# First loads and set-up of three attention programs: keys ahead of the bias, first queries from ScalarE's queue, second slot set up in the loop

## The chip, the core and the metric

The kernel runs on one core of a Trainium2 chip. The metric is the device time of one execution in microseconds (us); before the change it is 4377.17 us, the median of 3 runs from 4371.15 to 4381.04.

## What is computed

One step of a two-layer streaming encoder: 2048 frames of a new stream and 64 frames of a continued one. The first layer has 8 heads of group A (each chunk of 64 frames reads itself and eight chunks back, with a relative bias) and 8 heads of B (a frame reads all frames up to itself, with a forgetting term in the logits). The second has 8 heads of C (window of two chunks back, two key groups, a sink in the softmax) and 8 heads of D (one shared key and value, 256 selected keys for each frame).

```python
def attend(q, k, v, bias, mask, sink=None):
    s = jnp.einsum('bqhgd,bkhd->bhgqk', qg, k).astype(F32) * (d ** -0.5)
    s = s.reshape(b, hq, tq, -1) + bias
    s = jnp.where(mask, s, NEG_INF)
    ...
    o = jnp.einsum('bhgqk,bkhd->bqhgd', p, v)
...
    oa = chunk_band_prompt(qa, ka, va, A_BACK_CHUNKS, bias_a)
    ob = forget_prompt(qb, kb, vb, logf)
    mix = jnp.concatenate([oa * jax.nn.silu(ga), ob * jax.nn.silu(gb)], axis=-1)
    return x + mix @ w_out, new
```

## The kernel before

The kernel is a sequence of programs, with a barrier of all engines between two of them: projections, the attention of A and B (`attention_by_keys`), the output of the first layer, projections and selection of the second, the attention of C, then of D (`attention_by_blocks`, called once for each), and the output of the second layer. Each program writes what every engine does in its own order; engines wait for each other by counting semaphores. An engine runs its instructions in that order, so whatever stands behind a wait waits too. SP, ScalarE and GpSimd also issue DMAs, each on a queue of its own.

**A and B.** Sixteen heads run one after the other, each in one of two slots (`k_a`, `k_b`, `c_a`, `c_b`, `q_a`, `q_b`, `v`, `v_c`, with index head mod 2). A matrix of keys or queries is loaded as float32 into one of two `raw` buffers (`item_loads`: item 0 the keys, 1 the queries, 2 the cached keys, each in two halves of 64 partitions), rounded on ScalarE into the `_a` tile (`round_item`), and what rounding left is kept: for keys on GpSimd (`split_keys`, L859), for queries on VectorE (`split_queries`, a product into `q_b`, L848, and the remainder into `q_a`, L851). A score is then two matmuls. The rows 64 to 67 of the `_b` tiles hold ones that carry the softmax shift and the forgetting term. VectorE sets them up before the first head (L1166 to L1184): memsets of both slots, then, when the identity has come, `shown` and a product of each key tile with it (L1181), and a rounded identity (`ident_r`). Then it keeps the turned bias (`keep_bias`), and splits the first queries. TensorE turns the bias of a head against the identity (`turn_bias`), forms the maxima's scores (`maximum`, L951 and L952) into two banks, which VectorE reduces (`reduce`, L1112), and later the transposed scores (`scores`), which VectorE biases (`add_bias`), ScalarE exponentiates (`exponent`) and TensorE multiplies with the values (`values`). `KeyPlan` cuts this into chunks: the loop over `c` does scores two chunks ahead and maxima five.

**C and D.** Blocks of 128 queries, all heads of a block together. `key_loads` fills a `raw` buffer with the keys of one group (item 0), the cached keys (item 1), and for C the second group (2 and 3); items 2 and 3 wait until items 0 and 1 are split. `query_loads` loads one block of queries in four DMAs of 128 KB. VectorE waits for all three constants (identity, bias, and sinks in C or a bfloat16 identity in D: `consts` up to `N_CONST` = 48), keeps the turned bias (`keep_bias`), splits the first keys (`split_keys`, L1752) and then the queries. GpSimd issues the loads of the values once the tiles are set up (`fixed`), prepares a block (`prepare`, and for D `add_near`); in D it waits for the kept bias first.

## Time and profile before

| | before |
|---|---|
| median of 3 runs | 4377.17 us |
| lowest and highest | 4371.15 and 4381.04 us |
| the profiled execution, its own time | 4374.29 us |
| its span, first to last instruction | 4372.5 us |
| TensorE matmuls, busy | 3836.7 us, 88% of the span |
| VectorE, ScalarE, GpSimd, busy | 2250.8, 1593.5 and 682.4 us (51%, 36%, 16%) |
| granted TensorE clock, mean | 0.945 |

The profile is one execution. A busy share is an average over the whole span; the programs differ, so the heads of the programs are read from their own stretch. In the table by stretch the five busy times are those of TensorE's matmuls, its weight loads, VectorE, ScalarE and GpSimd, each with its instructions. An idle time stands in square brackets in a timeline row, with what ended it behind the arrow. The attention of A and B starts at 943.5 us of the span, that of C at 3164.5 and that of D at 3369.7.

### The profile page before, as it was taken

What the parts mean: (1) busy time and instruction counts of PE and PEld (TensorE: products, weight loads), DVE (VectorE), ACT (ScalarE), POOL (GpSimd) and SP (SyncE); (2) the same over time, 40 slices, a digit from 0 to 9 for tenths busy, and PEclk for the clock granted to TensorE, in tenths of its full rate; (3) what the DMA queues carried; (4) which work ended last, traced back from release to release, by engine and by line L of the source; (5) the groups of instructions that cost most, each with busy time, mean ns of one, the idle gap of its engine ahead of it and who ended that gap; (6) DMA issues with size and microseconds to landing.
All of it is one profiled execution on the core that took longest, in us unless ns stands there. A gap on an engine that the chain in (4) does not pass through costs nothing. (4 is left out here: it accounts for less than half of the span.)

```text
span 4372.5 us, 51419 instructions
## 1 busy us (share of the span) xinstructions
PE 3836.7 (88%) x18129; PEld 2643.7 (60%) x18129; DVE 2250.8 (51%) x4858; ACT 1593.5 (36%) x2424; POOL 682.4 (16%) x408
## 2 busy tenths in 40 slices
PE   5999999968888999996998779889877699999698
PEld 3789988966666566564874544443344455555376
DVE  7211111137776444443230199999678876666332
ACT  3100001104444334333320189995345333333333
POOL 3100000011212111111430000000032632211133
PEclk8999999989999999998999899999979799999899
DMA  5221122133334223212431211111243210100243
GB/s 184 69 73 67 63 73 81 65 84 82 92 91 99 63 60 74 64 36 91 160 126 63 63 38 57 56 58 48 80 104 94 61 39 23 25 21 3 97 154 125
DMA packets 222512, 328.51 MB, mean 75 GB/s; under 512 B 22224, under 2 KB 129032, under 8 KB 220896
## 3 DMA queue, kind: packets, MB, share of 16 engines
q1 hardware_dynamic: 173280, 236.21, 18.9%
q10 hardware_dynamic: 43776, 72.50, 4.5%
q0 software_dynamic: 5216, 16.70, 1.8%
q8 instruction: 138, 2.26, 0.2%
q14 instruction: 102, 0.84, 0.1%
HBM read 214.35 MB, written 110.99 MB: 74 GB/s over the span
## 5 line engine op out<-in xcount | busy, mean ns | idle before, releaser
L1017 PE MATMUL attAB_p_o<-attAB_pt,attAB_v 128*65 128x512 f32 (+3 forms) x1120 | 441.3, 492 | 3.0 <-ACT attAB_pt L1064 3.0
L1104 DVE TENSOR_REDUCE attAB_mx<-attAB_p_s 128x1 f32<-128x512 f32 (+2 forms) x360 | 210.7, 608 | 313.1 <-PE attAB_p_s L952 200.6
L497 DVE COPY ab_stage<-ab_pA 128x256 f32<-128x256 f32 (+1 forms) x108 | 56.5, 523 | 603.5 <-PE ab_pA L466 579.4
L2360 DVE TENSOR_SCALAR_CACHE_REDUCE cd_junk<-score,cd_thr 128x512 bf16<-128x512 f32 (+8 forms) x288 | 350.3, 1274 | 1.4 <-DVE cd_thr L2377 0.3
L2398 ACT ACTIVATE cd_gate<-score,cd_thr 128x384 bf16<-128x384 f32 (+2 forms) x192 | 322.3, 1679 | 23.3 <-DVE cd_thr L2377 16.1
L994 PE MATMUL attAB_p_t<-attAB_q_a,attAB_k_a 128*128 128x512 f32 (+3 forms) x560 | 314.0, 564 | 0.0
L464 PE MATMUL ab_pA<-ab_W_hi,h_hi 128*128 128x256 f32 x1088 | 309.0, 284 | 3.3 <-PE ab_pA L466 3.2
L465 PE MATMUL ab_pA<-ab_W_lo,h_hi 128*128 128x256 f32 x1088 | 307.9, 283 | 0.0
L466 PE MATMUL ab_pA<-ab_W_hi,h_lo 128*128 128x256 f32 x1088 | 307.8, 283 | 0.0
L495 ACT ACTIVATE ab_stage<-ab_pA 128x256 f32<-128x256 f32 (+1 forms) x108 | 50.1, 464 | 700.3 <-PE ab_pA L466 669.5
L1625 PE MATMUL attD_p_o<-attD_pt,attD_v 128*65 128x512 f32 x548 | 287.6, 606 | 0.0
L369 PE MATMUL cd_pA<-hT_cd,cd_W 128*128 128x512 f32 (+1 forms) x640 | 245.5, 544 | 39.0 <-ACT cd_stage L2561 26.7
L464 PE MATMUL ab_pA<-h_hi,ab_W_hi 128*128 128x512 f32 (+1 forms) x640 | 238.4, 373 | 14.1 <-ACTq L482 5.0
L372 PE MATMUL cd_pA<-cd_W,hT_cd 128*128 128x512 f32 x544 | 237.9, 599 | 13.7 <-ACT cd_stage L2561 13.3
L951 PE MATMUL attAB_p_s<-attAB_k_a,attAB_q_a 128*128 128x384 f32 (+3 forms) x560 | 209.1, 375 | 41.3 <-DVE attAB_mx L1112 22.1
L465 PE MATMUL ab_pA<-h_lo,ab_W_hi 128*128 128x512 f32 (+1 forms) x640 | 237.4, 371 | 0.0
L466 PE MATMUL ab_pA<-h_hi,ab_W_lo 128*128 128x512 f32 (+1 forms) x640 | 237.3, 371 | 0.0
L1603 PE MATMUL attD_p_t<-attD_q_a,attD_k_a 128*128 128x512 f32 x274 | 203.5, 743 | 26.1 <-DVE attD_s_t L1824 26.0
L1064 ACT ACTIVATE attAB_pt<-attAB_p_t 128x512 f32<-128x512 f32 (+2 forms) x328 | 175.9, 566 | 138.4 <-PE attAB_p_t L995 134.7
L2076 PE MATMUL mix_pY<-mix_W_hi,mix_m_hi 128*128 128x512 f32 x544 | 218.4, 402 | 0.0
L369 PEld LDWEIGHTS cd_pA<-hT_cd,cd_W 128*128 128x128 f32 x640 | 114.8, 197 | 169.7 <-issue 123.7
L2077 PE MATMUL mix_pY<-mix_W_lo,mix_m_hi 128*128 128x512 f32 x544 | 215.4, 396 | 0.0
(343 smaller groups left out, 8809.4 us busy)
## 6 DMA issues: line engine op xcount, KB each, us to landing
attAB_raw<-t_k SPq DMA_DIRECT2D x32, 640.0 KB, 7.3
attAB_raw<-t_q SPq DMA_DIRECT2D x32, 640.0 KB, 9.7
t_qg<-cd_stage SPq DMA_DIRECT2D x74, 256.0 KB, 2.0
ab_W_raw<-in_w_ab SPq DMA_DIRECT2D x17, 1024.0 KB, 5.8
mix_o<-t_o SPq DMA_DIRECT2D x34, 512.0 KB, 4.3
t_q<-ab_stage ACTq DMA_DIRECT2D x40, 256.0 KB, 2.0
t_k<-ab_stage ACTq DMA_DIRECT2D x40, 256.0 KB, 2.0
norm_x<-in_x ACTq DMA_DIRECT2D x17, 512.0 KB, 3.6
```

Of the source, the lines that this page charges most:

```text
L369: last = nc.tensor.matmul(pA[s][:, 0:w], W[j % 2][:, k, c * P:(c + 1) * P], hT[:, k, r * BANK:r * BANK + w], start=(k == 0), stop=(k == KT ...
L372: last = nc.tensor.matmul(pA[s][:, 0:w], hT[:, k, r * P:(r + 1) * P], W[j % 2][:, k, 0:w], start=(k == 0), stop=(k == KT - 1))
L464: nc.tensor.matmul(out, lh, rh, start=(k == 0), stop=False)
L465: nc.tensor.matmul(out, lh, rl, start=False, stop=False)
L466: last = nc.tensor.matmul(out, ll, rh, start=False, stop=(k == KT - 1))
L994: nc.tensor.matmul(out, hi[:, ks], q_a[j][:, cols], start=(x == 0), stop=False)
L1017: done = nc.tensor.matmul(p_o[u % 2][0:VW, i0 * P:(i0 + n) * P], left, pt[c % NPT][:, at * P:(at + n) * P], start=(c == plan.chunks_of[u][ ...
L1625: nc.tensor.matmul(p_o[u % 2][0:VW, :], left, pt[c % NPT][:], start=(c == first), stop=(c == last)).then_inc(valued, 1)
L2076: nc.tensor.matmul(out, m_hi[s][:, k, :], W_hi[:, k, cols], start=(k == 0), stop=False)
L2077: nc.tensor.matmul(out, m_hi[s][:, k, :], W_lo[:, k, cols], start=False, stop=False)
L2360: nc.vector.tensor_scalar(junk[nth % 2][:, 0:widths[n]], sc[n][:], T[:, n:n + 1], None, ALU.is_ge, ALU.add, accum_out=cnt[s % 2][:, n:n + ...
L2398: nc.scalar.activation(gate[:, 0:widths[n]], sc[n][:], ACT.Sign, bias=T[:, n:n + 1], accum_out=cnt[s % 2][:, n:n + 1]).then_inc(signed, 1)
```

## The change

In A and B, SP issues the identity and then the first keys, ahead of the first bias; the first queries are issued by ScalarE. VectorE sets up the first slot before the loop, with the rounded identity ahead of the key tiles' rest; the seven instructions for the second slot go into steps 0 to 5 of the loop (`fix_second`), and what reads the second slot waits for a new semaphore. TensorE turns the first bias before it waits for the set-up. In C and D, SP issues the first keys behind the identity and ahead of the bias and the third constant; the first two blocks of queries are issued by ScalarE, before its first wait.

```diff
--- before.py
+++ after.py
@@ -780,9 +780,10 @@
         row_turned, row_kept, bias_turned, bias_kept, bias_laid, t_biased = (sem(n) for n in (
             "row_turned", "row_kept", "bias_turned", "bias_kept", "bias_laid", "t_biased"))
         bias_in = [sem(f"bias_in{k}") for k in pair]
-        ident_in = sem("ident_in")
+        ident_in, second_fixed = sem("ident_in"), sem("second_fixed")
         ITEMS = 3
-        FIXED = 2 * 5 + 2 + 2 + 4
+        FIXED = 5 + 2 + 2 + 2
+        SECOND = 5 + 2
         span = lambda h: plan.last_of_head[h] + 1 - plan.first_of_head[h]
 
         places = {plan.first_of_head[h] + span(h) * (1 + 2 * n) // 9: (h + 1, n) for h in range(NH - 1) for n in range(ITEMS)}
@@ -844,6 +845,10 @@
         def split_queries(dve, h):
 
             j, m = h % 2, ITEMS * h + 1
+            if h == 0:
+                dve.wait_ge(fixed, FIXED)
+            if h == 1:
+                dve.wait_ge(second_fixed, SECOND)
             dve.wait_ge(rounded, m + 1)
             nc.vector.tensor_scalar(q_b[j][0:FORGET, :], q_a[j][0:FORGET, :].bitcast(F32), only_q[0:FORGET, 0:1], None,
                                     ALU.mult).then_inc(copied, 1)
@@ -877,11 +882,13 @@
             @block.sync
             def _(sp):
                 sp.dma_start(ident[:], d.ident).then_inc(ident_in, 16)
+                item_loads(sp, 0, 0)
                 for h in range(NH):
                     if kinds[h] == "A":
                         bias_loads(sp, h)
                     for n in range(ITEMS):
-                        item_loads(sp, h, n)
+                        if h or n == 2:
+                            item_loads(sp, h, n)
                         if h == 0 and n == 1:
                             for dst, src in ((identb, d.identb), (tri, d.tri), (tri_t, d.tri_t)):
                                 sp.dma_start(dst[:], src).then_inc(consts, 16)
@@ -929,6 +936,8 @@
                     if m == 0 or plan.units[plan.maxima[m - 1][0]][0] != h:
                         pe.wait_ge(k_split, 2 * h + 1)
                         pe.wait_ge(q_split, h + 1)
+                        if h == 1:
+                            pe.wait_ge(second_fixed, SECOND)
                         if h == HEADS:
                             pe.wait_ge(consts, 48)
                         if kinds[h] == "B":
@@ -1027,9 +1036,9 @@
                     done.then_inc(turned, 1)
 
                 pe.wait_ge(ident_in, 16)
+                turn_bias(0)
                 pe.wait_ge(fixed, FIXED)
                 pe.wait_ge(ident_kept, 2)
-                turn_bias(0)
                 for n, u in enumerate(plan.early):
                     for m in plan.max_of[u]:
                         maximum(m)
@@ -1078,6 +1087,7 @@
                         act.wait_ge(turned, u - 1)
                     nc.scalar.activation(o_t[u % 2][:, 0:w], p_o[u % 2][0:VW, 0:w], ACT.Copy).then_inc(o_kept, 1)
 
+                item_loads(act, 0, 1)
                 for n in range(ITEMS):
                     round_item(act, 0, n)
                 for u in plan.early:
@@ -1128,6 +1138,19 @@
                     dve.wait_ge(negated, 2 * u + 2)
                     nc.vector.tensor_tensor(lo, nm[u % 2][:, 0:n, :], hi.bitcast(F32), ALU.subtract).then_inc(shifted, 1)
 
+                def fix_second(x):
+
+                    if x < 3:
+                        nc.vector.memset((k_b, c_b, q_b)[x][1][HD:AUX, :].bitcast(F32), 1.0).then_inc(second_fixed, 1)
+                    elif x == 3:
+                        nc.vector.memset(v[1][:, :, HD:VW], 1.0).then_inc(second_fixed, 1)
+                        nc.vector.memset(v_c[1][:, :, HD:VW], 1.0).then_inc(second_fixed, 1)
+                    else:
+                        tile = (k_b, c_b)[x - 4]
+                        dve.wait_ge(second_fixed, x - 3)
+                        nc.vector.tensor_scalar(tile[1][HD:AUX, :], tile[1][HD:AUX, :].bitcast(F32), shown[HD:AUX, 0:1], None,
+                                                ALU.mult).then_inc(second_fixed, 1)
+
                 def keep_bias(h):
                     j = h % 2
                     for x, w in enumerate((BANK, P)):
@@ -1162,26 +1185,23 @@
                                             view[:, 0:n, 0:HD], rs[u % 2][:, 0:n, :].broadcast_to([P, n, HD]), ALU.mult
                                             ).then_inc(o_out, 1)
 
-                for j in pair:
-                    nc.vector.memset(k_b[j][HD:AUX, :].bitcast(F32), 1.0).then_inc(fixed, 1)
-                    nc.vector.memset(c_b[j][HD:AUX, :].bitcast(F32), 1.0).then_inc(fixed, 1)
-                    nc.vector.memset(q_b[j][HD:AUX, :].bitcast(F32), 1.0).then_inc(fixed, 1)
-                    nc.vector.memset(v[j][:, :, HD:VW], 1.0).then_inc(fixed, 1)
-                    nc.vector.memset(v_c[j][:, :, HD:VW], 1.0).then_inc(fixed, 1)
+                nc.vector.memset(k_b[0][HD:AUX, :].bitcast(F32), 1.0).then_inc(fixed, 1)
+                nc.vector.memset(q_b[0][HD:AUX, :].bitcast(F32), 1.0).then_inc(fixed, 1)
                 for k in pair:
                     nc.vector.memset(shift[k][:].bitcast(F32), 0.0).then_inc(fixed, 1)
                 nc.vector.memset(only_q[0:HD, :], 1.0).then_inc(fixed, 1)
                 nc.vector.memset(only_q[HD:AUX, :], 0.0).then_inc(fixed, 1)
                 dve.wait_ge(ident_in, 16)
+                nc.vector.tensor_copy(ident_r[:], ident[:]).then_inc(ident_kept, 1)
                 nc.vector.tensor_reduce(shown[HD:AUX, :], ident[HD:AUX, HD:FORGET], AX.X, ALU.max).then_inc(ident_kept, 1)
-                dve.wait_ge(ident_kept, 1)
-                dve.wait_ge(fixed, FIXED - 4)
-                for tile, w in ((k_b, ROWS), (c_b, WIDEST * P)):
-                    for j in pair:
-                        nc.vector.tensor_scalar(tile[j][HD:AUX, :], tile[j][HD:AUX, :].bitcast(F32), shown[HD:AUX, 0:1], None,
-                                                ALU.mult).then_inc(fixed, 1)
-                dve.wait_ge(fixed, FIXED)
-                nc.vector.tensor_copy(ident_r[:], ident[:]).then_inc(ident_kept, 1)
+                nc.vector.memset(c_b[0][HD:AUX, :].bitcast(F32), 1.0).then_inc(fixed, 1)
+                nc.vector.memset(v[0][:, :, HD:VW], 1.0).then_inc(fixed, 1)
+                nc.vector.memset(v_c[0][:, :, HD:VW], 1.0).then_inc(fixed, 1)
+                dve.wait_ge(ident_kept, 2)
+                dve.wait_ge(fixed, FIXED - 2)
+                for tile in (k_b, c_b):
+                    nc.vector.tensor_scalar(tile[0][HD:AUX, :], tile[0][HD:AUX, :].bitcast(F32), shown[HD:AUX, 0:1], None,
+                                            ALU.mult).then_inc(fixed, 1)
                 keep_bias(0)
                 split_queries(dve, 0)
                 for u in plan.early:
@@ -1193,6 +1213,8 @@
                 for c in range(NT):
                     if c + 2 < NT and kind_of(c + 2) == "A":
                         add_bias(c + 2)
+                    if c < 6:
+                        fix_second(c)
                     for m in plan.max_at[c]:
                         reduce(m)
                         if m == plan.max_of[plan.maxima[m][0]][-1]:
@@ -1436,17 +1458,15 @@
             @block.sync
             def _(sp):
                 sp.dma_start(ident[:], d.ident).then_inc(consts, 16)
+                key_loads(sp, 0)
                 sp.dma_start(bias[:], (d.bias_c if kind == "C" else d.bias_d).rearrange("h p n -> p h n")).then_inc(consts, 16)
                 if kind == "C":
                     sp.dma_start(sink[:], d.sinks.broadcast_to([P, HEADS])).then_inc(consts, 16)
                 else:
                     sp.dma_start(identb[:], d.identb).then_inc(consts, 16)
-                key_loads(sp, 0)
-                query_loads(sp, 0)
                 if kind == "D":
                     for b in range(NMASK):
                         mask_loads(sp, b)
-                query_loads(sp, 1)
                 for m in range(1, len(items)):
                     key_loads(sp, m)
                 for b in range(2, NRAW - 1):
@@ -1716,6 +1736,8 @@
                         act.wait_ge(turned, u - 1)
                     nc.scalar.activation(o_t[u % 2][:], p_o[u % 2][0:VW, :], ACT.Copy).then_inc(o_kept, 1)
 
+                query_loads(act, 0)
+                query_loads(act, 1)
                 act.wait_ge(fixed, FIXED)
                 round_keys(0)
                 for b in plan.early_blocks:
```

## Rows read from the trace of the kernel before

**Rows 1.** Table by stretch: window, length, five busy times, granted clock, DMA share, GB/s.
```profile
944.00:975.00 31.00, 1.30 (x5) 0.93 (x5) 27.07 (x24) 4.66 (x3) 12.66 (x7) 0.50 0.63 142
...
3164.00:3200.00 36.00, 6.99 (x31) 6.46 (x31) 16.91 (x36) 6.66 (x6) 11.48 (x9) 0.50 0.82 181
...
3369.00:3400.00 31.00, 4.82 (x22) 4.01 (x22) 16.15 (x16) 6.13 (x6) 11.95 (x7) 0.50 1.01 210
```

**Rows 2.** Timeline, head of A and B: start, duration, engine, line, out<-in, [idle before].
```profile
956.03 2.02 ACT L842 ACTIVATE attAB_k_a<-attAB_raw 128x2176 fp32r<-128x2176 f32 x1 [18.53 <-DMA attAB_raw<-t_k]
...
958.13 4.75 POOL L859 TENSOR_TENSOR attAB_k_b<-attAB_raw,attAB_k_a 64x2176 fp32r<-64x2176 f32 x1 [10.10 <-ACT attAB_k_a L842]
...
963.40 2.02 ACT L842 ACTIVATE attAB_q_a<-attAB_raw 128x2176 fp32r<-128x2176 f32 x1 [5.35 <-DMA attAB_raw<-t_q]
...
967.72 1.17 DVE L1184 CAST attAB_ident_r<-attAB_ident 128x128 fp32r<-128x128 f32 x1
...
972.48 2.61 DVE L851 SCALAR_TENSOR_TENSOR attAB_q_a<-attAB_raw,attAB_q_a 64x2176 fp32r<-64x2176 f32 x1
...
975.19 0.45 PE L951 MATMUL attAB_p_s<-attAB_k_a,attAB_q_a 128*128 128x128 f32 x1 [4.71 <-DVE attAB_q_a L851]
```

**Rows 3.** Timeline, A and B: long memsets of the set-up, idle times in the loop.
```profile
946.33 1.76 DVE L1167 MEMSET attAB_c_b<- 4x2048 f32 x1 [0.38 <-issue]
...
948.50 1.87 DVE L1168 MEMSET attAB_q_b<- 4x2176 f32 x1 [0.40 <-issue]
...
992.94 0.69 DVE L1148 TENSOR_TENSOR attAB_s_t<-attAB_p_t,attAB_bias_t 128x512 f32<-128x512 f32 x1 [2.15 <-PE attAB_p_t L995]
...
997.31 0.39 PE L951 MATMUL attAB_p_s<-attAB_k_a,attAB_q_a 128*128 128x256 f32 x1 [0.61 <-DVE attAB_mx L1112]
```

**Rows 4.** Lines L1181 and L848 by themselves: durations in ns, least/median/most, first and last start.
```profile
L1181 DVE TENSOR_SCALAR attAB_k_b<-attAB_k_b,attAB_shown x2: 1337/3474/5612, 958.4 to 964.0; 4x2176 fp32r<-4x2176 f32 x2
...
L848 DVE TENSOR_SCALAR attAB_q_b<-attAB_q_a,attAB_only_q x16: 1339/1342/1346, 971.1 to 1914.2; 66x2176 fp32r<-66x2176 f32 x16
```

**Rows 5.** DMA queues (packets, MB, share): 3155 to 3215 (GpSimd's), then 3179 to 3183.
```profile
q0 software_dynamic: 416, 1.18, 9.0%
...
q0 software_dynamic: 256, 0.79, 89.0%
q1 hardware_dynamic: 255, 0.12, 18.2%
```

**Rows 6.** Timeline, head of C, in the order of time.
```profile
3171.95 0.23 DVE L1854 CAST attC_ident_r<-attC_ident 128x128 fp32r<-128x128 f32 x1 [1.36 <-DMA attC_sink<-in_sinks]
...
3176.01 0.69 DVE L1765 COPY attC_bias_t<-attC_p_o 128x512 f32<-128x512 f32 x1 [0.16 <-PE attC_p_o L1540]
3177.91 2.02 ACT L1673 ACTIVATE attC_k_a<-attC_raw 128x2176 fp32r<-128x2176 f32 x1 [17.18 <-DMA attC_raw<-t_kq]
...
3182.40 1.28 SPq L1391 DMA_DIRECT2D attC_raw<-t_kq  x2
...
3194.02 2.02 ACT L1673 ACTIVATE attC_k_a<-attC_raw 128x2176 fp32r<-128x2176 f32 x1 [4.85 <-DMA attC_raw<-t_kq]
...
3198.63 0.45 PE L1577 MATMUL attC_p_s<-attC_k_a,attC_q_a 128*128 128x128 f32 x1 [5.69 <-DVE attC_k_b L1752]
```

**Rows 7.** Timeline, head of D, in the order of time.
```profile
3376.24 0.49 DVE L1854 CAST attD_ident_r<-attD_ident 128x128 fp32r<-128x128 f32 x1 [1.07 <-DMA attD_identb<-in_identb]
...
3384.39 2.42 DVE L1752 TENSOR_TENSOR attD_k_b<-attD_raw,attD_k_a 64x2176 fp32r<-64x2176 f32 x1 [3.13 <-ACT attD_k_a L1673]
...
3391.00 2.84 POOL L1471 TENSOR_SCALAR attD_q_b<-attD_q_a,attD_only_q 66x1024 fp32r<-66x1024 f32 x1 [12.57 <-ACT attD_q_a L1679]
...
3393.87 14.76 DVE L1758 SCALAR_TENSOR_TENSOR attD_q_a<-attD_q_raw,attD_q_a 64x1024 fp32r<-64x1024 f32 x2 [7.06 <-POOL attD_q_b L1471]
...
3403.35 7.25 POOL L1489 TENSOR_TENSOR attD_near_t<-attD_bias_t,attD_msk_t 128x1024 f32<-128x1024 f32 x3
...
3412.68 0.27 DVE L1788 CUSTOM_DVE_ANT_0 attD_junk<-attD_p_s,attD_near 128x128 bf16<-128x128 f32 x1
```

## The prediction

> **What bounds the kernel now.** By the page TensorE is busy 88% of the span, so in the long stretches the time is TensorE's, and a change at the head of a program counts by when its first matmuls of scores can run. I read the table by stretch at the three heads next [rows 1]: in the heads of A and B, of C, and of D TensorE does 1.30, 6.99 and 4.82 us of work in 31, 36 and 31 us, at a granted clock of 0.50 (the 1.2 GHz level; it had idled). VectorE is busy 27.07 of 31 us in the first, but 16.91 of 36 and 16.15 of 31 in the others, and there transfers fill the time (DMA share 0.82 and 1.01, 181 and 210 GB/s). Last, the timeline at each head.
>
> A and B [rows 2]: keys are rounded on ScalarE at 956.03, when they have landed, queries at 963.40. VectorE's set-up ends only with the cast at 967.72, so the turned bias, the split of the queries (972.48, 2.61 us) and the first matmul of scores (975.19) are late because of VectorE.
>
> C [rows 6]: the constants are there at 3171.95, the last turned bias is kept by 3176.70, and only then do the keys come (3177.91). When VectorE has split them, SP issues the keys of the second group into the freed buffer (3182.40); they are rounded at 3194.02, and TensorE goes on with the second unit at 3198.63. That load is the bound. D [rows 7]: constants at 3376.24; GpSimd starts its preparation at 3391.00 and works on to 3410.60; VectorE, held up beside it, comes to the first maximum at 3412.68.
>
> **The change part by part.** *Queries on ScalarE's queue.* They move from behind the keys to beside them. The price depends on how two queues share the DMA engines. In 4 us in which SP's and GpSimd's queues were both full, one moved 255 packets (0.12 MB), the other 256 (0.79 MB) [rows 5]: they take turns packet by packet, whatever the size. So I let ScalarE's queue add no rate and take turns with SP's, at the 210 GB/s of D's saturated head [rows 1]. By the code's access patterns the keys are 640 packets of 2 KB (1.31 MB), C's and D's two blocks of queries 2048 of 512 bytes (1.05 MB), their bias 1024 of 1 KB (1.05 MB); C's values are 416 packets, 1.18 MB [rows 5].
>
> The issues on ScalarE (two in A and B, eight in C and D, of some 0.65 us, as SP's pair of 1.28 [rows 6]) I cost at nothing: rounding waits for landed keys, and in C and D the bias comes later still. Without that cover they are 5.2 us at most. SP keeps the rest of its order; D's cached keys come one place earlier and are needed last.
>
> *Bias behind the keys, in C.* VectorE runs in order: it waits for all constants, keeps the bias, then splits the keys. Before, the bias came first and was kept 1.2 us ahead of the keys [rows 6]: free. After: the stream begins near 3166.2; the keys' 640 packets with as many of the queries are 1.64 MB, 7.8 us, so the keys land near 3174. Then 1024 packets of bias pass with 1024 of the queries and, since the values are in full turn by 3179 [rows 5], with all 416 of those: 1.05 + 0.52 + 1.18 = 2.75 MB, 13.1 us: constants near 3187. From there 4.75 us as before (3171.95 to 3176.70) and a split of 2.42 us (the same instruction in [rows 7]): buffer free at 3194.2, not 3182.4. The second group's load then finds idle engines: 1.31 MB are 6.2 us, with issue and latency some 8 us (an estimate; in the crowd of before it took 11.6), so 3202, 8 us later than 3194.02. Bounds: with the values behind the bias 1.57 MB, 7.5 us, give constants at 3181.5 and 2.7 us; with 11.6 us for the load again, 11.8 us. I take **+8**.
>
> *In D.* Keys land near 3379, but bias and identity at 3379.2 + 2.65 MB / 210 GB/s = 3392, for 3376.24. With 4.8 us as in C, GpSimd starts near 3396.8, not 3391.00, and its 19.6 us of work move by 5.8. The split of the keys (2.42 us, before in free time at 3384.39) now falls beside GpSimd, where two instructions of half that length took 14.76 us [rows 7]. Bounds: +0.6 with the values behind the bias, +8.2 with the whole split added. I take **+6**, near the shift alone, because VectorE's last pieces run after GpSimd's end either way.
>
> *A and B, head.* VectorE now sets up the first slot alone, before the loop: one of each pair of memsets and of products with the shown column goes, and the one product that ran beside GpSimd (5.61 us [rows 4]) with its hold. It is free near 956 instead of 968.9, and transfers end last: keys, queries and values are 3.29 MB, 15.7 us from 945.3, so keys and queries land together near 961 (keys 5 us later than before, queries 2.4 earlier). The bias follows 1.6 us behind and is kept by 964.7: no delay, as TensorE turns it ahead of its wait for the set-up. Keys are rounded by 963.1, queries by 965.1, and GpSimd splits the keys from 963.2 to 967.9 (its 4.75 us [rows 2]). Here VectorE's product for the queries meets GpSimd's subtraction. In all 16 heads of before it took 1.34 us; another product of its kind took 5.61 us instead of 1.34 [rows 4] when it ran beside exactly this GpSimd instruction. So I let it end at 969.2; the 2.61 us follow, and the first matmul comes at 971.9: **−3.3**. Without the hold, 969.2: −6.
>
> The Trainium skill ("SBUF — State Buffer", on the shared port pair) says that VectorE and GpSimd take that pair under an exclusive lock for a whole instruction while the other waits; by it the sum has the −3.3, by the sixteen rows the −6. The trace agrees with it in the 5.61 us.
>
> *Second slot inside the loop.* Three long memsets, two of 0.07 and two products: 1.87 + 1.76 + 1.87 + 0.14 + 2 x 1.34, with some 0.4 us of issue before each long memset [rows 3, 4], are 9.5 us. They now stand in VectorE's order between a bias addition and the maxima of steps 0 to 5. The maxima behind them free TensorE's banks, and TensorE already waits for them there (0.61 us), while VectorE has a single long idle time of 2.15 us [rows 3]. The first memset fits into that; the other 7.2 us meet two engines that wait for each other in turn. Bounds: 0, if all is taken up, and 9.5. I take **+4.5**, the middle, since neither row decides. The new waits (VectorE and TensorE for the second slot's semaphore) are over long before head 1 and cost nothing.
>
> **Sum.** −3.3 + 4.5 + 8 + 6 = +15.2 us on the profiled execution's own 4374.29 us: 4389.5, so 4389. The median shown lies 2.9 us above that execution; the range allows for it.
>
> **The rivals.** (1) *The values come behind the bias:* C +2.7, D +0.6, A and B +1.2: 4379. For it: no row fixes the values' first packet; against: 1024 packets of bias need longer than the few us of head start. (2) *The loop takes up the set-up and the hold isn't met:* A and B −6, C and D +14: 4382. For it: VectorE isn't full there; against: TensorE's waits for the maxima. (3) *Faster: ScalarE's queue brings a rate of its own.* Each queue then runs at 210 GB/s. In A and B keys land at 951.5, VectorE's set-up (956) bounds and the first matmul comes near 962, −13, of which the loop takes 4.5: −8.5. In C keys land at 3172.4 and the bias at 3177.4; the buffer is free 2 us later, but the second load meets emptier engines: 0. In D the bias lands at 3382.6 and GpSimd starts at 3387.4: −3.6. Together −12: 4362. It decides if the two hardware queues together move over 300 GB/s into the raw buffers. Against it stands the turn-taking [rows 5], though that is GpSimd's queue beside SP's, not ScalarE's.
>
> The Trainium skill ("DMA: Bandwidth & Descriptors", "Issuing engines are not separate DMA queues") says that such transfers run on the same sixteen engines and save issue time alone; by it rival (3) falls.
>
> **How the numbers follow.** Forecast 0.56, rival (1) 0.14, (2) 0.18, (3) 0.12. About 0.2% (8.8 us) is what a measurement of this kernel can tell from no change. With all terms at their upper bounds the forecast is 26 us above (4400, and 4403 with the median's 2.9); rivals (1) and (2) together are 3 us below. A little of the forecast lies within 0.2%, and so do (1) and (2): slower 0.52, same 0.36, faster 0.12. The range leaves out (3) and the far ends: 4374 to 4402.
>
> **What would show it.** Right: in C the cast of the identity some 15 us later after the program's start than now, the second keys issued near 3194 and rounded near 3202; in D GpSimd's first product 5 to 6 us later; in A and B the first matmul 3 to 4 us earlier, with memsets between the maxima and longer TensorE waits for them. Wrong: constants in C within 10 us of the keys' issue, keys that land in 6 us with queries beside them, or a loop in A and B as short as before.

## The result, and the profile after

| | before | after |
|---|---|---|
| median, us | 4377.17 | 4398.15 (4395.07 to 4411.51) |
| ratio to before | 1 | 1.0058, 95% interval 1.0043 to 1.0072 |
| profiled execution: time, span, us | 4374.29, 4372.5 | 4411.51, 4409.7 |
| first load of A and B to their last output, us | 1091.6 | 1112.8 |
| the same for C, D, us | 202.1, 737.7 | 212.4, 742.0 |

Slower, on the side I forecast, but by 21 us where the forecast (4389) lay 12 above the median. Executions of the changed kernel lie in two groups, 4395 to 4398 and 4410 to 4412, and the profiled one is of the upper; the ratio, which comes to 25 us, weighs both. In the lower group the loss is about 20 us; what lifts the other executions by some 14 us more is a question of its own, to which the experiments come back. The last three lengths are worked out from SP's first load and VectorE's last output of a program.

Head of A and B after, timeline (start, duration, engine, line, out<-in, idle before), for [rows 2, 4]:

```profile
960.12 2.02 ACT L843 ACTIVATE attAB_k_a<-attAB_raw 128x2176 fp32r<-128x2176 f32 x1 [23.53 <-DMA attAB_raw<-t_k]
...
962.05 2.00 ACT L843 ACTIVATE attAB_q_a<-attAB_raw 128x2176 fp32r<-128x2176 f32 x1
...
962.23 4.77 POOL L864 TENSOR_TENSOR attAB_k_b<-attAB_raw,attAB_k_a 64x2176 fp32r<-64x2176 f32 x1 [15.12 <-ACT attAB_k_a L843]
964.15 3.99 DVE L853 TENSOR_SCALAR attAB_q_b<-attAB_q_a,attAB_only_q 66x2176 fp32r<-66x2176 f32 x1 [1.06 <-ACT attAB_q_a L843]
...
970.86 0.44 PE L960 MATMUL attAB_p_s<-attAB_k_a,attAB_q_a 128*128 128x128 f32 x1 [8.48 <-DVE attAB_q_a L856]
```

Keys and queries land together near 960, VectorE's product is held beside GpSimd's subtraction (3.99 us instead of 1.34), and the first matmul of scores comes 28.2 us after SP's first load, where it came after 31.6. That head went as forecast. Then the loop, first VectorE's timeline, then TensorE's waits in the same stretch, for [rows 3]:

```profile
985.98 1.87 DVE L1144 MEMSET attAB_k_b<- 4x2176 f32 x1 [0.51 <-issue]
...
989.88 1.76 DVE L1144 MEMSET attAB_c_b<- 4x2048 f32 x1 [0.48 <-issue]
...
995.95 0.69 DVE L1171 TENSOR_TENSOR attAB_s_t<-attAB_p_t,attAB_bias_t 128x512 f32<-128x512 f32 x1 [2.07 <-PE attAB_p_t L1004]
997.14 1.87 DVE L1144 MEMSET attAB_q_b<- 4x2176 f32 x1 [0.51 <-issue]
...
1005.77 0.69 DVE L1171 TENSOR_TENSOR attAB_s_t<-attAB_p_t,attAB_bias_t 128x512 f32<-128x512 f32 x1 [2.28 <-PE attAB_p_t L1004]
1006.50 1.34 DVE L1151 TENSOR_SCALAR attAB_k_b<-attAB_k_b,attAB_shown 4x2176 fp32r<-4x2176 f32 x1
```

```profile
992.30 0.66 PE L960 MATMUL attAB_p_s<-attAB_k_a,attAB_q_a 128*128 128x384 f32 x1 [2.73 <-DVE attAB_mx L1122]
999.53 0.58 PE L960 MATMUL attAB_p_s<-attAB_k_a,attAB_q_a 128*128 128x256 f32 x1 [3.07 <-DVE attAB_mx L1122]
1008.45 0.43 PE L973 MATMUL attAB_p_s<-attAB_ident_r,attAB_shift 128*66 128x128 f32 x4 [1.98 <-DVE attAB_mx L1122]
```

Behind three of the five long pieces TensorE waits 2 to 3 us for a maximum, where 0.61 was the pattern. VectorE's own long idle times (2.07 and 2.28 us, waits for TensorE's transposed scores) are still there: they stand ahead of the bias additions, and the pieces come behind these in its order. The table of the stretch 985 to 1012 (length, busy PE, PEld, DVE, ACT, POOL, granted clock, DMA share, GB/s), before and then after:

```profile
985.00:1012.00 27.00, 23.75 (x110) 17.53 (x110) 18.60 (x54) 13.34 (x18) 4.83 (x1) 0.85 0.29 65
```

```profile
985.00:1012.00 27.00, 19.22 (x61) 12.98 (x61) 16.89 (x40) 7.65 (x10) 4.79 (x1) 0.69 0.12 28
```

61 matmuls instead of 110, at a mean granted clock of 0.69 instead of 0.85: the engine that is made to wait also falls back to its 1.2 GHz level. The last output of head 0, before and then after:

```profile
1044.44 0.22 DVE L1161 TENSOR_TENSOR attAB_o<-attAB_p_x,attAB_rs 128x64 f32<-128x64 f32 x1
```

```profile
1051.09 0.22 DVE L1184 TENSOR_TENSOR attAB_o<-attAB_p_x,attAB_rs 128x64 f32<-128x64 f32 x1
```

Head 0 ends 108.7 us after the first load, before 101.1: with a start 3.4 us earlier, the loop lost 11 us.

Head of C after, timeline, for [rows 6], and the table of four of its stretches:

```profile
3198.09 2.02 ACT L1693 ACTIVATE attC_k_a<-attC_raw 128x2176 fp32r<-128x2176 f32 x1 [15.15 <-DMA attC_raw<-t_kq]
...
3208.91 0.23 DVE L1876 CAST attC_ident_r<-attC_ident 128x128 fp32r<-128x128 f32 x1 [16.11 <-DMA attC_sink<-in_sinks]
...
3213.58 2.41 DVE L1774 TENSOR_TENSOR attC_k_b<-attC_raw,attC_k_a 64x2176 fp32r<-64x2176 f32 x1
3216.01 1.29 SPq L1413 DMA_DIRECT2D attC_raw<-t_kq  x2
...
3224.61 2.02 ACT L1693 ACTIVATE attC_k_a<-attC_raw 128x2176 fp32r<-128x2176 f32 x1 [13.75 <-DMA attC_raw<-t_kq]
```

```profile
3187.00:3199.00 12.00, 0.00 (x0) 0.00 (x0) 4.79 (x12) 0.91 (x1) 4.55 (x6) 0.50 0.99 207
3199.00:3210.00 11.00, 0.71 (x4) 0.75 (x5) 0.38 (x3) 2.45 (x3) 2.85 (x1) 0.50 0.92 203
3210.00:3216.00 6.00, 2.93 (x14) 2.53 (x12) 5.09 (x5) 0.86 (x2) 2.84 (x1) 0.50 0.00 0
3216.00:3226.00 10.00, 1.97 (x8) 1.78 (x8) 2.65 (x3) 1.39 (x1) 0.00 (x0) 0.50 0.91 190
```

The program starts at 3186.7. The first keys are rounded at 3198.09, but VectorE stands 16.11 us at the wait for the constants, keeps the bias and splits the keys only at 3213.58. From 3210 to 3216 the DMA engines move nothing (share 0.00): all that could be issued has landed, and the one load that is wanted waits for its buffer.

Head of D after (start 3402.3), timeline, for [rows 7]:

```profile
3423.33 0.23 DVE L1876 CAST attD_ident_r<-attD_ident 128x128 fp32r<-128x128 f32 x1 [15.66 <-DMA attD_identb<-in_identb]
...
3428.00 2.40 DVE L1774 TENSOR_TENSOR attD_k_b<-attD_raw,attD_k_a 64x2176 fp32r<-64x2176 f32 x1
3428.26 4.86 POOL L1491 TENSOR_SCALAR attD_q_b<-attD_q_a,attD_only_q 66x1024 fp32r<-66x1024 f32 x1 [17.32 <-DVE attD_bias_t L1787]
...
3449.28 0.27 DVE L1810 CUSTOM_DVE_ANT_0 attD_junk<-attD_p_s,attD_near 128x128 bf16<-128x128 f32 x1
```

GpSimd begins 26.0 us after the start (before 21.2), the first maximum comes at 47.0 (before 42.9).

### The profile page after: what moved, and what is told of

Its sections match the earlier page's. It is cut to its first block and busy times, and to the rows that moved or that the text cites. A ratio compares the mean times of both kernels' runs of the same rounds, so it can differ in the third digit from the quotient of the medians.

```text
span 4409.7 us, 51422 instructions
## 1 busy us (share of the span) xinstructions
PE 3848.7 (87%) x18129; PEld 2647.2 (60%) x18129; DVE 2247.3 (51%) x4858; ACT 1593.3 (36%) x2424; POOL 681.1 (15%) x408
## 5 line engine op out<-in xcount | busy, mean ns | idle before, releaser
L1026 PE MATMUL attAB_p_o<-attAB_pt,attAB_v 128*65 128x512 f32 (+3 forms) x1120 | 451.2, 501 | 3.0 <-ACT attAB_pt L1073 3.0
L1114 DVE TENSOR_REDUCE attAB_mx<-attAB_p_s 128x1 f32<-128x512 f32 (+2 forms) x360 | 211.1, 609 | 324.1 <-PE attAB_p_s L961 209.8
L372 PE MATMUL cd_pA<-cd_W,hT_cd 128*128 128x512 f32 x544 | 237.3, 598 | 15.1 <-ACT cd_stage L2583 14.8
```

Of the source, the lines that this page charges most:

```text
L372: last = nc.tensor.matmul(pA[s][:, 0:w], hT[:, k, r * P:(r + 1) * P], W[j % 2][:, k, 0:w], start=(k == 0), stop=(k == KT - 1))
L1026: done = nc.tensor.matmul(p_o[u % 2][0:VW, i0 * P:(i0 + n) * P], left, pt[c % NPT][:, at * P:(at + n) * P], start=(c == plan.chunks_of[u][ ...
```

## The experiments

Ratios are to the kernel before on the same chip (medians 4376.8 to 4377.5), with 95% intervals. "Start" is SP's first load of the program in question.

**Each half alone.** A and B as changed, C and D as before; then the reverse.

> The kernel before with the change in A and B alone (C and D as before). Theory one, the set-up in the loop costs more than I forecast: the two traces put the end of head 0 7.6 us later though the first matmul of scores came 3.4 us earlier, so 11 us for the loop, and this kernel takes +7 us on the kernel before (ratio 1.0015 to 1.002). Rival, the forecast's size: -3.3 + 4.5 = +1 us (1.000 to 1.0005), and the missing time lies in C and D. A third outcome, +20 us, would say that the drops of the granted clock in heads 7 to 14 that the profiled execution of the changed kernel shows belong to the change in A and B and to most executions.

> The kernel before with the change in C and D alone. If the parts add as the two traces show them, C takes 10 us longer and D 4: +14 us (ratio about 1.0033), which is also what I forecast (+8 and +6). Rival: the change in C and D costs more than the traces show, +20 us or more, and A and B nothing.

Measured: 4386.05 (1.0024, 1.0015 to 1.0033), +8.6 us, and 4389.24 (1.0032, 1.0020 to 1.0044), +11.8 us. Together 20.4: the two halves add up to the lower group of the changed kernel. C and D cost what I forecast (+14) less 2; A and B do not.

**The set-up ahead of the loop.**

```diff
+                for x in range(6):
+                    fix_second(x)
                 keep_bias(0)
...
-                    if c < 6:
-                        fix_second(c)
```

> C and D as before; A and B as changed, but the second slot is set up before the loop, behind the first slot's set-up and ahead of the turned bias, where VectorE waits 8.7 us for the bias. Theory one (the set-up's place in the loop costs 11 us): the head keeps its 3.4 us gain and the loop is as short as before, so -3 us on the kernel before (ratio 0.9993), 10 us less than the run with the change in A and B alone. Rival (the order of the loads, or the earlier start, makes the loop longer): the first output comes late here too, +5 us or more.

Measured: 4374.29 (0.9996, 0.9987 to 1.0005). The last output of head 0, in e1 (start 942.0) and then here (start 941.6):

```profile
1051.49 0.23 DVE L1184 TENSOR_TENSOR attAB_o<-attAB_p_x,attAB_rs 128x64 f32<-128x64 f32 x1
```

```profile
1038.07 0.23 DVE L1184 TENSOR_TENSOR attAB_o<-attAB_p_x,attAB_rs 128x64 f32<-128x64 f32 x1
```

Head 0 ends 96.7 us after the start, against 109.7 in e1 (98.4 to 98.7 in the five later profiles with these A and B: e11 to e14 and e18). With the same loads and the same instructions, the place alone is worth 11.8 us between the medians. The head, timeline:

```profile
959.44 1.34 DVE L1151 TENSOR_SCALAR attAB_k_b<-attAB_k_b,attAB_shown 4x2176 fp32r<-4x2176 f32 x1
...
962.01 0.89 DVE L1161 COPY attAB_bias_t<-attAB_p_s 128x512 f32<-128x512 f32 x2
...
963.21 4.54 DVE L853 TENSOR_SCALAR attAB_q_b<-attAB_q_a,attAB_only_q 66x2176 fp32r<-66x2176 f32 x1 [0.32 <-ACT attAB_q_a L843]
...
970.47 0.45 PE L960 MATMUL attAB_p_s<-attAB_k_a,attAB_q_a 128*128 128x128 f32 x1 [9.07 <-DVE attAB_q_a L856]
```

The seven instructions fit into the idle time before the bias; the first matmul comes 28.8 us after the start.

**How the loop's cost goes with place and amount.** In e5 the six pieces stand later (at steps 6, 8, 10, 11, 12 and 13, the queries' memset first); in e6 the memsets stand ahead and only the two products in the loop (`if c in (4, 5)`).

> C and D as before; A and B as changed, but the six pieces of the second slot's set-up stand at steps 6, 8, 10, 11, 12 and 13 of the loop instead of 0 to 5. The same 9.5 us of VectorE. Theory one (the cost comes from the place: in the first steps TensorE waits for nearly every maximum, at the lower level of its clock, and the exponents of step 3 to 5 moved from 50.1, 55.2, 59.4 to 46.8, 59.0, 66.8 us after the start): at the later steps VectorE has more room, and the run is at most 3 us above the kernel before, 5 us or more under the run with steps 0 to 5 (4386.05). Rival (VectorE bounds the whole of head 0, so each us costs a us wherever it stands): as the run with steps 0 to 5, +8 us.

> C and D as before; A and B as changed, but the second slot's memsets stand ahead of the loop and only its two products (2 x 1.34 us, with issue some 3 us) stay at steps 4 and 5. Theory one, as far as the cost goes with the work (about 11 us for 9.5 of VectorE): +3 us on the run with all of it ahead (4374.29), so near 4377. Rival: the first pieces do the harm and the products lie beside other work: as with all ahead, 4374; or the place does the harm, whatever the work: +6 us and more, 4380.

Measured: 4390.75 (1.0029, 1.0019 to 1.0039), so my first theory fell: later steps are no cheaper than the first. TensorE's waits of e5:

```profile
1005.56 0.69 PE L961 MATMUL attAB_p_s<-attAB_k_a,attAB_q_a 128*128 128x384 f32 x1 [1.91 <-DVE attAB_mx L1123]
...
1019.46 0.48 PE L986 MATMUL attAB_p_s<-attAB_ident,attAB_bias 128*128 128x128 f32 x1 [4.80 <-DVE attAB_mx L1123]
1029.31 0.39 PE L961 MATMUL attAB_p_s<-attAB_k_a,attAB_q_a 128*128 128x128 f32 x1 [3.61 <-DVE attAB_c_b L1152]
```

The last, 3.61 us, is the changed kernel's own new wait for the second slot, which e5 made late; without it e5 is about like e1. e6 gave 4382.37 (1.0012, 1.0001 to 1.0022), with half of its executions at 4375 to 4379 and half at 4386 to 4391. The profiled one (4377.77) is 2.6 us above that of e3 (4375.21), and its head 0 ends at 101.3, 4.6 us later than in e3's profile and 2.6 to 2.9 later than in the five others: roughly in proportion to the 2.7 us of work. What puts the other half 10 us higher its profile can't show.

**Work of no use in a later head.** As e3, with three memsets and two products on a scratch tile in the first six steps of head 4 or of head 12.

```diff
+                    if 0 <= c - plan.first_of_head[4] < 6:
+                        spend(c - plan.first_of_head[4])
```

> The run with the second slot set up ahead of the loop (4374.29), and in the first six steps of head 4 (an A head in mid-run) VectorE does work of no use beside its own: three memsets and two products of 4x1920 (some 1.65 and 1.2 us each, 7.3 us, 8.5 with issue). Theory one (in an A head VectorE, 36.8 to 37.8 us busy in 50, and TensorE wait for each other in turn, so a us of VectorE costs a us and more): +9 to +12 us. Rival (only the start of head 0, where nothing is buffered yet, is so tight): +3 us at most.

> The same work of no use in the first six steps of head 12, a B head, where VectorE is 38.2 us busy in 82 and TensorE 77.9, at the 2.4 GHz level throughout. Theory one: VectorE has room and only maxima wait: +0 to +3 us over the run with the second slot ahead (4374.29). Rival, any VectorE work between maxima stops TensorE: +9 us, as in head 4.

Measured: 4384.75 (1.0018, 1.0009 to 1.0027) and 4383.32 (1.0018, 1.0009 to 1.0027): +10.5 and +9.0 us on e3's median, which is of another chip (by the ratios 9.6 each). In A as expected. In B the rival won: a busy share of 47% was no room. Table of 1717 to 1735 in e3 and then e10, and one line of e10's VectorE:

```profile
1717.00:1735.00 18.00, 16.24 (x78) 10.36 (x77) 11.31 (x20) 6.50 (x10) 4.82 (x1) 1.00 0.57 129
```

```profile
1717.00:1735.00 18.00, 13.33 (x56) 7.49 (x54) 16.46 (x21) 5.50 (x9) 6.90 (x4) 0.98 0.44 98
```

```profile
1726.89 5.07 DVE L1165 TENSOR_SCALAR attAB_scratch<-attAB_scratch,attAB_shown 4x1920 fp32r<-4x1920 f32 x1
```

At the head's start VectorE was already busy 11.31 of 18 us and goes to 16.46; TensorE falls from 16.24 to 13.33. One product took 5.07 us instead of 1.21, as GpSimd worked beside it, so 11 us of VectorE cost 9 there. In both runs TensorE's granted clock also fell at these steps, for 6.8 us from 1734.1 in e10 (not at all in e3) and for 13.7 us from 1195.0 in e9 (3.4 in e3), so part of the cost is the clock's.

**C and D: the order and the queue apart.** In e7 the bias goes first as before and only the queries move to ScalarE's queue; in e8 the keys go first and the queries stay behind the bias on SP's.

```diff
 e7, against before
-                query_loads(sp, 0)
...
-                query_loads(sp, 1)
...
+                query_loads(act, 0)
+                query_loads(act, 1)
                 act.wait_ge(fixed, FIXED)
 e8, against before
                 sp.dma_start(ident[:], d.ident).then_inc(consts, 16)
+                key_loads(sp, 0)
...
-                key_loads(sp, 0)
                 query_loads(sp, 0)
```

> A and B as before; in C and D the bias goes first as before and only the queries move to ScalarE's queue. Theory (two queues take turns packet by packet and add no rate): the bias lands 2.5 us later (1024 packets of 1 KB with as many of 512 bytes), the keys some 3 us; C +3, D +3: about +6 us. Rival, the queue has a rate of its own: bias as early as before, queries up to 5 us earlier: C 0, D -3.

> A and B as before; in C and D the keys go first but the queries stay on SP's queue, behind the bias. Theory: the constants are there some 7 us earlier than with the queries beside them (15 us after the start, not 22), VectorE's split ends near 23 (18 before, 29 after the change), C +5; D about 0 to +2, as its queries land as before and bound GpSimd: about +6 us in all, so that the order and the queue have about half of the 12 us each. Rival, the order alone costs all of it: +12 us.

Measured: 4378.35 (0.9998, 0.9989 to 1.0006) and 4375.21 (0.9994, 0.9986 to 1.0003). Both expectations of +6 fell, and yet the two together are +11.8. In e7 the first keys of C are rounded 3.1 us later than before, as expected, but the constants come only 0.8 later and not 2.5. The load of the second keys in C tells why. e7, timeline (start 3164.5), then e8 (start 3164.7):

```profile
3185.48 1.28 SPq L1391 DMA_DIRECT2D attC_raw<-t_kq  x2
3193.91 2.02 ACT L1671 ACTIVATE attC_k_a<-attC_raw 128x2176 fp32r<-128x2176 f32 x1 [6.54 <-DMA attC_raw<-t_kq]
```

```profile
3184.71 1.29 SPq L1391 DMA_DIRECT2D attC_raw<-t_kq  x2
3193.54 2.02 ACT L1673 ACTIVATE attC_k_a<-attC_raw 128x2176 fp32r<-128x2176 f32 x1 [4.68 <-DMA attC_raw<-t_kq]
```

Issued at 21.0 and 20.0 us after the start, it is rounded 8.4 and 8.8 us on, at 29.5 and 28.8; before, issued at 17.9, it took 11.6 us in the crowd and was rounded at 29.5. A few us of delay at the issue are taken back by emptier engines. After the whole change it is issued at 29.3, takes the same 8.6 us, and nothing is left to take back. So order and queue each use up the same slack.

**The split ahead of the wait for the constants.**

```diff
                 dve.wait_ge(fixed, FIXED)
+                split_keys(0)
                 dve.wait_ge(consts, N_CONST)
...
                 keep_bias()
-                split_keys(0)
```

> A and B as before; C and D as changed, but VectorE splits the first keys before it waits for the constants. Theory: C is late because the split stands behind the wait for the bias and so holds SP's load of the second group's keys; here the split ends some 16 us after the program's start (18 before, 29 after the change), the load is issued then, and C is within 2 us of before, while D keeps its +4 us because GpSimd waits for the bias in any case: +4 us in all (ratio 1.001). Rival: the late bias itself holds C (the maxima and the turned bias need it), C keeps its +10 us: +14 us in all (1.0033).

Measured: 4377.74 (1.0003, 0.9994 to 1.0012). C's timeline (start 3162.0):

```profile
3176.89 1.29 SPq L1391 DMA_DIRECT2D attC_raw<-t_kq  x2
...
3183.45 0.23 DVE L1855 CAST attC_ident_r<-attC_ident 128x128 fp32r<-128x128 f32 x1 [6.59 <-DMA attC_sink<-in_sinks]
...
3189.51 2.02 ACT L1671 ACTIVATE attC_k_a<-attC_raw 128x2176 fp32r<-128x2176 f32 x1 [2.68 <-DMA attC_raw<-t_kq]
```

The constants are nearly as late as in the changed kernel (21.5 us after the start), the second keys are rounded at 27.6, and C is 202.2 us long (202.1 before; 211.1 in e2). The late bias by itself costs C nothing; that the split stands behind it is the whole cost. D, whose GpSimd waits for the bias in any case, is 742.9 us long in this profile (737.7 before); the median shows nothing of the +4 us expected for it, though its interval reaches 5.

**Both causes undone in the changed kernel**: e3's and e4's moves, all loads as changed.

> The changed kernel, all its loads as they are, with two things moved in VectorE's order: the second slot's set-up from the loop to ahead of the turned bias in A and B, and the split of the first keys ahead of the wait for the constants in C and D. Theory (the two causes are all of the loss): -3 from A and B, 0 in C, +2 to +4 in D: 4374 to 4379 with the kernel before at 4377, 20 us under the changed kernel (4398.15). Rival (a third cost that only the whole change has): 4385 or more.

Measured: 4384.89 (1.0013, 1.0004 to 1.0021), but in two groups again, 4374 to 4376 and 4385 to 4388. The lower is the theory's 4374 to 4379. The median is the rival's: seven of the twelve lie in the upper group, and by the ratio this kernel is still 6 us slower than the one before. For the gap, two more profiles:

> The changed kernel once more, for a profile. Theory (drops of the granted clock in the B heads part its executions): a time near 4396 comes with B heads 82 us long and one stretch of some 669 us at the 2.4 GHz level, and A and B some 13 us shorter than the 1112.8 of the first profile; a time near 4410 comes with the drops again. Rival: near 4396 with the drops, or near 4410 without.

> The kernel of e13 once more, for a profile. Theory: a time near 4386 comes with drops of the granted clock in B heads that are longer than 82 us, 11 us in sum; a time near 4375 with none, as in the first profile. Rival: near 4386 without drops in the B heads, the 11 us elsewhere.

They gave 4412.20 and 4372.66, each again of the group that already had a profile. The table of one B stretch, in the changed kernel (4411.51) and in e1 (4386.05):

```profile
1655.00:1740.00 85.00, 80.88 (x389) 51.72 (x388) 38.15 (x73) 32.11 (x54) 12.27 (x5) 0.96 0.26 56
```

```profile
1655.00:1740.00 85.00, 80.88 (x405) 51.66 (x403) 41.18 (x76) 32.65 (x56) 15.34 (x6) 1.00 0.27 57
```

With the same A and B, TensorE is as busy but does 389 instead of 405 matmuls, as its granted clock drops to the lower level twice, for 3.4 us each. Such drops in B's heads stand in both profiles of the changed kernel (A and B 1112.8 and 1112.1 us, e1 1101.2) and in that of e14 (1099.1, e13 1091.3); the other profiles have none or one. Up to the end of head 7 the changed kernel and e1 take the same time (462 us from the start); then a B head takes 82 us without a drop, 83.6 with one and 85.1 to 85.2 with two, so its seven drops (from 1436.1 to 1855.9) make up nearly all of the 11.6 us between 1112.8 and 1101.2. The mean granted clock of whole executions parts the changed kernel's groups too (0.943 to 0.945 in the lower, 0.936 to 0.941 in the upper), but not those of e13 (0.941 to 0.947 and 0.941 to 0.944). No lower-group execution of the changed kernel and no upper one of e13 was profiled, so that the drops part the groups is likely, not shown, and what sets them off is open.

**What can be gained.** e11 is e3's A and B with e8's C and D; e12 has the values' loads behind GpSimd's preparation as well; e14 is e13 with late values; e15 is e3 with all loads of A and B on SP's queue; e16 is e15's A and B with e12's C and D.

```diff
 e12, C and D
-                for g in kvs:
-                    value_loads(pool, g)
...
+                for g in kvs:
+                    value_loads(pool, g)
                 if kind == "C":
                     for u in plan.early:
 e15, A and B
-                item_loads(sp, 0, 0)
...
-                        if h or n == 2:
-                            item_loads(sp, h, n)
+                        item_loads(sp, h, n)
...
-                item_loads(act, 0, 1)
```

> A and B with the second slot set up ahead of the loop, C and D with the keys first and the queries left on SP's queue. If the two parts add: 3 us and 2 us under the kernel before, 4372 (ratio 0.9985 to 0.9995). Rival: the parts don't add, because the phase of the clock's changes at the head of C moves with the end of B (C was 205.1 us long in the first of the two, 202.1 before): as before, 4377.

> As the last, but in C and D GpSimd issues the values' loads after its preparation of the queries and not at the program's start. Theory, from the runs with one half of the change in C (second keys rounded 27.6 to 29.5 us after the start, whether issued at 14.9 or at 21.0): all that is issued by then shares the sixteen engines, and the second keys land when the sum of bytes is through; without 1.18 MB of values in C (5.6 us at 210 GB/s) they are rounded near 24, and C is up to 4 us shorter: 4367 to 4371. Rival: what comes next (the split of the second block of queries ends at 29.6 in any case) holds C where it is, and the values come late for the first product with them: 4372 to 4377.

> As the last, with the values' loads in C and D behind GpSimd's preparation of the queries. Theory (bytes on the sixteen engines bound the heads of C and D): without 1.18 MB of values ahead of them the second keys of C land 5 us earlier and the bias of D too, so 4 to 6 us under the last run, 4370 to 4374. Rival (the bias behind the keys holds D in any case): no more than 2 us under it.

> C and D as before; in A and B the identity first and both slots set up before the loop in the new order, but all loads on SP's queue as before (bias, keys, queries). Theory (the queries beside the keys cost some 2 us: both land near 960 to 962, where in the old order keys are rounded at 956.03 and queries at 963.40): the queries' split can start at 965.4, 3 us before the run with queries on ScalarE's queue; the first matmul of scores comes some 26 us after the start (31.6 before, 29 with the queries beside the keys), 4369 to 4373. Rival (VectorE's products for the second slot meet GpSimd's split of the keys, 958.1 to 962.9, and are held as one was before, 5.61 us): first matmul near 29, 4373 to 4377, no better than the run with queries on ScalarE's queue (4374.29).

> A and B as in the last run, C and D with the keys first, queries on SP's queue and the values behind GpSimd's preparation. If the parts add: 2 to 4 us under the run with late values and A and B of e3 (4372.56), 4368 to 4371, ratio 0.998 to 0.9988 to the kernel before. Rival: A and B gain nothing over it, 4372 to 4374.

Measured: e11 4376.72 (1.0001, 0.9992 to 1.0010): the small gains of e3 and e8, neither clear of the noise, did not add. e12 4372.56 (0.9991, 0.9982 to 1.0000), but not by the expected way: C's second keys are rounded at 28.7, not 24; D's GpSimd starts 17.9 us after the start (20.7 in e8), and D is shorter, 733.3. e14 4372.19 (0.9992, 0.9982 to 1.0003), 12.7 under e13's median, of which the groups hide how much is the values'. e15 4373.05 (0.9987, 0.9978 to 0.9996). Its head:

```profile
961.04 2.50 DVE L1148 TENSOR_SCALAR attAB_k_b<-attAB_k_b,attAB_shown 4x2176 fp32r<-4x2176 f32 x1
...
967.07 3.86 DVE L856 SCALAR_TENSOR_TENSOR attAB_q_a<-attAB_raw,attAB_q_a 64x2176 fp32r<-64x2176 f32 x1
...
971.19 0.45 PE L958 MATMUL attAB_p_s<-attAB_k_a,attAB_q_a 128*128 128x128 f32 x1 [22.99 <-DVE attAB_q_a L856]
```

The rival held there: VectorE meets GpSimd in other places (2.50 for 1.34, 3.86 for 2.42), and the first matmul is 28.0 us after the start, little better than e3's 28.8. So by the first matmul the queries' queue is worth 0.9 us in A and B; the intervals of the two ratios overlap. e16 gave 4369.15 (0.9986, 0.9977 to 0.9995), 6 us under the kernel before by the ratio and 29 under the changed one: the lowest median, and faster than both, but by the ratios not to be told from e15.

## Why the prediction missed

*Head of A and B, −3.3:* right up to the first matmul, −3.4, and by its steps: landing together near 960 (forecast 961), the product held (3.99 us), the first matmul from the queries' split. By the Trainium skill's rule on the shared port pair ("SBUF — State Buffer", "Who interferes with whom") the term was −3.3, and the trace of after agrees with that in the 3.99 us. That the gain reaches the end is not shown: with the set-up out of the loop head 0 ends at 98.4 to 98.7 in the profiles of e11, e12, e13 and e18, for 101.1 before, but A and B take 1091.3 to 1092.1 us in them, as in the profiles with A and B as before (1091.2 to 1092.1), and only e3's own profile is shorter (1087.2).

*Second slot in the loop, +4.5:* this step failed. It measured 11 us between the traces, 11.8 between the medians of e1 and e3, and 11.0 to 13.0 at the end of head 0 between e1 and the six profiles with e3's A and B; the upper bound was 9.5. (The ratios of e1 and e3 leave 5 to 6 us on either side, so by the time alone the bound isn't excluded; the middle is.) "I take the middle, since neither row decides" let VectorE's idle time count as room. It was not: the idle times stand ahead of the bias additions and the pieces behind them, and VectorE works in order, so a 1.87 us memset holds every maximum behind it, and TensorE waits for three of them (2 to 3 us in place of 0.61). The sum also had no term for TensorE's clock: the mean of the stretch 985 to 1012 fell from 0.85 to 0.69. That is the likely reason why the cost exceeds the work; no run parts it from the waits. e5, e9 and e10 show that this holds at later steps and in later heads, 0.8 us or more for each us of VectorE; e6, with less work, shows it only in that its median is higher.

*C, +8:* mechanism and marks right (constants 14.8 us later, second keys rounded 8.4 us later, as forecast), the size +10.3 in that execution, whose clock reached its higher level for good at 65.3 us after the start instead of 54.2, and +9.0 and +8.3 in the profiles of e2 and e17 with the same C (61.1 and 61.8). By the median both C and D together are +11.8 where I had +14. What the sum did not see is that the term exists only when both halves are there.

*D, +6:* +4.3 in that execution, +7.0 and +8.3 in e2 and e17 with the same D, while D as before takes 736.6 to 740.2 us: the mechanism is right and the size about right. The shift of GpSimd was 4.7, not 5.8, and the first maximum moved 4.1.

*Base:* the sum was made on 4374.29, 2.9 us under the median of before; that alone is a third of the shortfall, and the range had it.

*Rivals:* (1) fell with the constants at 22.2 us after the start. (2) fell on both of its conditions. (3), a rate of its own for ScalarE's queue, fell: the head of C runs at 207 and 203 GB/s with ScalarE's queue beside SP's, where D's head before had 210 without it [rows 1]. The Trainium skill ("DMA: Bandwidth & Descriptors", "Issuing engines are not separate DMA queues") said so, and the trace agrees.

## What to carry to other kernels

Set-up moved off a head into a loop can be paid nearly in full, or more, if it goes onto an in-order engine whose results another engine waits for in each step, even where that engine is busy for only 47% of a head; an idle time is room only for what stands ahead of its wait in the engine's order. Look for one long enough before the loop (here 8.7 us before the bias). Before a load goes ahead of another, look at what the consumer waits for first: keys loaded first gained nothing while their split stood behind the wait for the bias. Two delays on one path may each be free and cost 12 us together; after a forecast sum, ask which terms share a slack.

## What the runs showed of the hardware

- C's second keys, a load of 1.31 MB, took 8.4 to 9.0 us from issue to its consumer where the engines moved at most 0.4 MB beside it (after, e2, e7, e8, e12), and 11.6 and 12.6 where they moved 0.9 and 1.4 MB (before, e4).
- The same instructions of A and B took 1101.2 us in e1 and 1112 to 1113 us in the two profiles of the changed kernel, where TensorE's granted clock fell to the 1.2 GHz level for 3.4 us at a time inside heads in which it was 95% busy. No row here tells what sets that off.
- C, the same instruction for instruction, took 201.9 to 202.5 us where the granted clock first rose for 3.4 us at 40 us after the start (before, e1, e5, e10), and 203.5 to 205.1 where it did so at 11 us or not at all before 54 (e3, e6, e9, e15). A difference of up to 3 us in the length of C in one execution therefore says little.
